# On-chip tensors begun at multiples of 512 bytes by fill words, in a fused two-block transformer kernel

## What is computed

```python
def swiglu(x, w1, w3, w2):
    return (jax.nn.silu(x @ w1) * (x @ w3)) @ w2

def moe_swiglu(x, router_w, w1, w3, w2):
    ...
    logits = (xt @ router_w).astype(jnp.float32)
    top_vals, top_idx = lax.top_k(logits, TOP_K)
    ...
    for e in range(N_EXPERTS):
        out = out + combine[:, e:e + 1] * swiglu(xt, w1[e], w3[e], w2[e])
```

## The kernel before

| tile | before | after |
|---|---|---|
| `raw`, `whi`, `wlo`, `h`, `tok`, `xh`, `xl`, `con` | 128 | 0 |
| `kc2`, `xw`, `bias` | 416 | 0 |
| `qT`, `kT`, `vs`, `ob`, `sg`, `pT`, `zt`, `postg` | 288 | 0 |
| `qk`, `sq` | 416 | 0 |
| `v2`, `qkT`, `uT` | 32 | 0 |
| `cv`, `mixT`, `mixs`, `spa`, `spb`, `wT` | 64 | 0 |
| `gt`, `ht`, `pt_in`, `hTh`, `hTl`, `ptTh`, `ptTl`, `pg`, `pm` | 416 | 0 |
| `mTh`, `mTl`, `xnh`, `xnl`, `xgh`, `xgl`, `yh`, `yl`, `pick`, `pickT` | 416 | 0 |
| `kd`, `xwh` | 352 | 64 |
| `xwl` | 128 | 352 |
| `cmpa`, `cmpb` | 480 | 64 |

## Time and profile before

### The profile page before, as it was taken

One profiled execution on the slowest core, in us unless ns is written; L12 is line 12 of the kernel. 1 busy time (PEld: TensorE's weight loads), 2 busy tenths in 40 slices (PEclk: granted clock), 3 DMA queues, 4 the chain that ended last, 5 costly groups with the idle time before them and its releaser, 6 DMA issues.

```text
span 1925.3 us, 26803 instructions
## 1 busy us (share of the span) xinstructions
PE 1838.6 (95%) x9562; PEld 1546.2 (80%) x9562; DVE 1395.7 (72%) x1653; ACT 1220.0 (63%) x1536; POOL 5.9 (0%) x13
## 2 busy tenths in 40 slices
PE   8999979989999989879999999999999999999997
PEld 7877758979998779768878878788788787887885
DVE  4456755746664466458899898898998898989884
ACT  5545544644444455548687777786877777768773
POOL 0000000000000000000000000000000000000000
PEclk9889989999999999879999999999999999999999
DMA  9743223425445344219989899899898998998980
GB/s 321 248 165 109 74 102 131 154 100 190 177 190 202 111 175 176 93 67 339 369 319 362 317 364 364 310 367 355 325 361 319 352 360 325 358 345 343 357 323 23
DMA packets 68336, 483.32 MB, mean 251 GB/s; under 512 B 7610, under 2 KB 7738, under 8 KB 10928
## 3 DMA queue, kind: packets, MB, share of 16 engines
q1 hardware_dynamic: 66480, 475.26, 64.9%
q0 software_dynamic: 1792, 7.18, 1.8%
HBM read 478.22 MB, written 4.19 MB: 251 GB/s over the span
## 4 chain that ended last, share of the span: by engine, by line
PE 80%; DVE 8%; ACT 6%; issue 5%; DMA 0%; ACTq 0%; DVEq 0%; POOLq 0%
PE ps L1471 20%; PE ps L1472 19%; PE ps L1476 19%; DVE wlo L892 4%; PE ps L1716 4%; PE ps L1723 4%; PE ps L1717 4%; PE ps L1454 3%; ACT whi L549 2%; PE ps L1928 1%; PE ps L1929 1%; ACT xgh L846 1%; DVE sg L1015 1%; ACT sg L672 1%; PE ps L1819 1%
## 5 line engine op out<-in xcount | busy, mean ns | idle before, releaser
L892 DVE TENSOR_TENSOR wlo<-raw,whi 128x1024 fp32r<-128x1024 f32 x906 | 1044.1, 1212 | 171.8 <-ACT whi L549 171.3
L549 ACT ACTIVATE whi<-raw 128x1024 fp32r<-128x1024 f32 x906 | 904.2, 1055 | 154.6 <-PE ps L1476 127.4
L1471 PE MATMUL ps<-whi,xgh 128*128 128x512 f32 x896 | 360.2, 402 | 4.6 <-ACT whi L549 4.6
L1472 PE MATMUL ps<-whi,xgl 128*128 128x512 f32 x896 | 355.0, 396 | 0.0
L1476 PE MATMUL ps<-wlo,xgh 128*128 128x512 f32 x896 | 282.2, 396 | 0.0
L1471 PE MATMUL ps<-whi,xh 128*128 128x512 f32 (+1 forms) x448 | 186.9, 418 | 21.9 <-issue 9.9
L1471 PEld LDWEIGHTS ps<-whi,xgh 128*128 128x128 f32 x896 | 168.9, 188 | 43.1 <-ACT whi L549 4.8
L1476 PEld LDWEIGHTS ps<-wlo,xgh 128*128 128x128 f32 x896 | 168.9, 188 | 40.8
L1472 PEld LDWEIGHTS ps<-whi,xgl 128*128 128x128 f32 x896 | 169.2, 189 | 37.8
L1472 PE MATMUL ps<-whi,xl 128*128 128x512 f32 (+1 forms) x448 | 181.3, 406 | 0.0
L1471 PE MATMUL ps<-whi,mTh 128*128 128x512 f32 x448 | 178.3, 398 | 0.0
(11 more groups left out here) (288 smaller groups left out, 1902.5 us busy)
## 6 DMA issues: line engine op xcount, KB each, us to landing
raw<-in_w_moe_dram SPq DMA_DIRECT2D x336, 1024.0 KB, 6.7
raw<-in_w_fixed_dram SPq DMA_DIRECT2D x112, 1024.0 KB, 4.9
bias_scratch<-revb POOLq DMA_DIRECT2D x1, 3072.0 KB, 39.2
bias<-bias_scratch POOLq DMA_DIRECT2D x1, 2048.0 KB, 18.2
raw<-in_w_fixed_dram SPq DMA_DIRECT2D x4, 512.0 KB, 4.2
tok<-in_xt_dram SPq DMA_DIRECT2D x2, 512.0 KB, 4.5
h<-in_x_dram SPq DMA_DIRECT2D x1, 1024.0 KB, 13.6
out_dram<-h SPq DMA_DIRECT2D x2, 512.0 KB, 2.8
```

The source lines that it names most:

```text
L549: AC(whi[:, v % SPL, c], raw[:, v % RAW, c], ACT.Copy).then_inc(high_done, 1)
L892: V.tensor_tensor(wlo[:, v % SPL, c], raw[:, v % RAW, c], whi[:, v % SPL, c].bitcast(F32), ALU.subtract).then_inc(low_done, 1)
L1471: mm(o, hi(k0 + k, T), wh[:, k, :], start=first and k == 0, stop=False)
L1472: mm(o, lo(k0 + k, T), wh[:, k, :], start=False, stop=False)
```

## The change

A helper `fill` allocates a tile that nothing uses, as long as is missing to the next multiple of 512 bytes. It is called at four places: ahead of `raw`, after `con`, after the small tiles common to all stages, and after the small tiles of the attention stage. `cbias`, `cu` and `qk_ss`, whose sizes are no multiples of 512, are allocated later than before, behind the large tiles of their scopes. All engines run the same instructions in the same order, on other addresses.

```diff
--- before.py
+++ after.py
@@ -47,6 +47,8 @@
 
 SMALL_PARTS = (("gains", 7 * KD), ("square", 7 * P), ("tril", 64), ("diag", 8), ("ogain", 2 * KD), ("qkg", 4),
                ("convw", 32), ("rw", KD * NE))
+LINE = 512
+FRONT = 16512
 SMALL = {}
 SMALL_WORDS = 0
 for _name, _n in SMALL_PARTS:
@@ -136,6 +138,12 @@
         def sb(name, shape, dt=F32, scope=ctx):
             return scope.enter_context(nc.sbuf_tensor(name, shape, dt))
 
+        def fill(name, used, scope=ctx):
+            used = -(-used // 32) * 32
+            if used % LINE:
+                sb(name, [P, (LINE - used % LINE) // 4], scope=scope)
+
+        fill("front", FRONT)
         raw = sb("raw", [P, RAW, KU * NB])
         whi = sb("whi", [P, SPL, KU * NB], F32R)
         wlo = sb("wlo", [P, SPL, KU * NB], F32R)
@@ -144,6 +152,7 @@
         xh = sb("xh", [P, KD, S], F32R)
         xl = sb("xl", [P, KD, S], F32R)
         con = sb("con", [P, SMALL_WORDS])
+        fill("con_end", 4 * SMALL_WORDS)
 
         def part(name):
             a, n = SMALL[name]
@@ -161,6 +170,7 @@
         st = sb("st", [P, 64])
         epst = sb("epst", [P, 1])
         nround = sb("nround", [1, 1], I32)
+        fill("common_end", 512 + 256 + 32 + 32)
 
 
         with ExitStack() as nsa:
@@ -172,10 +182,10 @@
                 xw = sb("xw", [P, XT], scope=a)
 
             bias = sb("bias", [P, NH, S], scope=nsa)
-            cbias = sb("cbias", [P, NT, NH, NC_], scope=nsa)
             qT = sb("qT", [P, NH // 2, S], scope=nsa)
             kT = sb("kT", [P, 2, NG, S], scope=nsa)
             vs = sb("vs", [P, 2, NT, NG * DH], scope=nsa)
+            cbias = sb("cbias", [P, NT, NH, NC_], scope=nsa)
             cmpw = sb("cmpw", [P, CB + 6 * DH], scope=nsa)
             pos2 = cmpw[:, 0:CB].rearrange("p (a m) -> p a m", a=2)
             w2k = cmpw[:, CB:CB + 4 * DH].rearrange("p (j s d) -> p j s d", j=2, s=2)
@@ -185,6 +195,8 @@
             cst = sb("cst", [P, 3, NT * NH], scope=nsa)
             grow = sb("grow", [P, NT, NH], scope=nsa)
             ast_ = sb("ast", [P, 16, 3, RG], scope=nsa)
+            fill("nsa_end", 4 * (NT * NH * NC_ + CB + 6 * DH + NG * NC_ + NT * 3 * NH + 3 * NT * NH + NT * NH
+                                 + 16 * 3 * RG) + 16, scope=nsa)
             with ExitStack() as early:
                 with ExitStack() as a:
                     oh = sb("oh", [NBUCK + 1, 512 + LREV + NH], scope=a)
@@ -215,11 +227,9 @@
         with ExitStack() as mx:
             qk = sb("qk", [P, 2, NT, NB], scope=mx)
             sq = sb("sq", [P, NT, NB], scope=mx)
-            qk_ss = sb("qk_ss", [P, 2, NT, SH], scope=mx)
             v2 = sb("v2", [P, NT, NB], scope=mx)
             qkT = sb("qkT", [P, 2, 4, S], scope=mx)
             uT = sb("uT", [P, 4, S], scope=mx)
-            cu = sb("cu", [P, 4, S + 2], scope=mx)
             cv = sb("cv", [P, 4, S], scope=mx)
             mixT = sb("mixT", [P, 8, S], scope=mx)
             mixs = sb("mixs", [P, 8, S], scope=mx)
@@ -228,6 +238,8 @@
             spa = sb("spa", [P, 4, 3 * P], scope=mx)
             spb = sb("spb", [P, 4, 3 * P], scope=mx)
             wT = sb("wT", [P, 4, 3 * P], scope=mx)
+            cu = sb("cu", [P, 4, S + 2], scope=mx)
+            qk_ss = sb("qk_ss", [P, 2, NT, SH], scope=mx)
 
 
         with ExitStack() as ff:
```

## The result

The changed kernel takes 1904.54 us (median of 4 runs, 1902.64 to 1906.22). The kernel before, run again beside it, takes 1923.38 (4 runs, 1921.16 to 1926.49). The ratio is 0.9898, with an interval of 0.9885 to 0.9911, so 18.8 us are gone, clear of the interval. The forecast was 1899.4 and a ratio of 0.989. Against the 1921.33 shown ahead of the prediction, which three runs gave, the 1904.54 lies 0.9% lower. The profiled executions differ by a little more: 1927.16 before, 1906.07 after (span 1904.3), 21.1 us.

The account below looks back on a forecast made before the run. The prediction took TensorE's stream as the bound (95% busy, 80% of the chain). Expert loop 19.4, dense w2 2.2 and `ple` 0.3 sum to 21.9 us, taking 1921.33 to 1899.4 us; range 1893 to 1923.

Parts of the forecast that it names:

- 1.36 and 2.72 between the groups: Sign: `wlo` matmul groups 1.36 us apart in the expert loop instead of 1.40, 2.72 in dense w2 instead of 2.80.
- 2.72 in the `xh` blocks still: Sign: 12 matmuls with stationary tile `xh`/`xl` keep taking 2.72 us, as before the change.
- 0.96 us for eight of `unit_T`: Sign: eight `unit_T` matmuls, with stationary tile `whi`/`wlo`, keep taking 0.96 us.
- the condition: In `products`: a stationary tile 32 bytes off a 64-byte multiple, the moving tile not, costs 6.67 ns per matmul.
- Rival 2: Address 0 is a bad start, so `xh`/`xl` and `unit_T` matmuls slow by 21.4 us, to 1942.7; chance 0.07.
- rival 3: Full multiple removes another 6.67 ns of the 13.3 above 213.3 everywhere, 45.8 us more, to 1853.6; chance 0.04.
- The expert loop: Eight rounds of 127.68 us, each 2.4 us shorter after the restart cost, 19.4 us in all.
- 96 matmuls after the gather: VectorE sets the end there, so 0.64 us won on PE returns as a longer wait for `yl`: nothing.
- The restarts: After transposes in the expert loop, nine a round, streams take time to settle: 0.3 us a round, between 0 and 1.0.
- From the scatter to the next gather's end, 408 matmuls, PE is held by no one: In each expert round, 408 matmuls at 6.67 ns gain 2.72 us, since VectorE still idles in each hidden block.
- Dense w2: 336 matmuls with `hTh`/`hTl`, PE busy 50.0 of 50 us, at 6.67 ns each: 2.2 us gained.
- `ple`: Two stages of 24 matmuls each with `ptTh`/`ptTl`, the last work on PE there: 0.3 us, nothing if hidden.

Follow-up runs that it names:

- E1: Changed kernel with the stationary tiles moved to 32 bytes past a multiple of 512, weight rings left at 0: 1923.69 us, ratio to before 0.9996.
- E2: Changed kernel with 32 bytes more fill ahead of all tiles, so stationary and moving tiles both begin at 32: 1904.96 us, ratio to before 0.9902.
- E4: Changed kernel with the weight rings, `xh` and `xl` moved to 32, stationary tiles of expert loop and dense w2 at 0: 1922.41 us.
- E3: Kernel before with 32 bytes of fill ahead of `gt`, stationary tiles at 448, rings at 128, distance 320: 1923.01 us, ratio to before 0.9996.
- E5: Changed kernel with `hTh` 256, `xgh` 128, `mTh` 64 and `ptTh` 16 bytes from the rings, which stay at 0: 1921.85 us, one run.
- E8: Changed kernel with VectorE's split of the round's last unit moved behind the two `yl` instructions: 1900.73 us, ratio to before 0.9877.
- E9: Changed kernel with VectorE's `pick` made earlier and its last split moved behind the two `yl`: 1893.94 us, ratio to before 0.9839.

## Why the prediction was right

**The mechanism.** The reading of the trace of before held: one form of matmul took 226.7 ns in one stage and 233.3 in another, and what sorted them was an address. All signs that the prediction named came: 1.36 and 2.72 between the groups, 2.72 in the `xh` blocks still, 0.96 us for eight of `unit_T`, 1219 and 1060 ns on VectorE and ScalarE, and the 16 transposes in 1.91 us. The round is 125.60 us, where about 125.3 was named. E1, E2 and E4 show the cause, which before was argued from three stages only. What the prediction had wrong is the condition. It blamed a stationary tile "32 bytes off a 64-byte multiple while the moving tile doesn't"; E3 and E5 show that distances of 64, 128 or 320, all multiples of 64, are as slow. Both conditions give the same answer for this change, since it puts everything at 0. That the number didn't suffer from the wrong condition is luck. For a change that had set the tiles at 64-byte multiples, the same reasoning would have missed by the whole gain, as E3 does.

**Rival 2 (0 is a bad start)** and **rival 3 (a full multiple gives still more)** have fallen with the same rows: the `xh` blocks go from 128, 128 to 0, 0 and stay at 2.72, `unit_T` stays at 0.96, and E2 reaches the time of after with everything at 32.

**The expert loop.** Forecast 2.4 us a round, measured 2.07 (seven rounds), 16.6 in eight where 19.4 was forecast. The terms, each by its own row:
- 96 matmuls after the gather gain nothing: right. VectorE's stretch kept its length, gather to scatter is 27.01 us as before, and the wait for `yl` went to 1.36 us, forecast 1.4. E8 confirms it from the other side: relieve VectorE there of one unit's split (2.27 us), and 0.91 us a round comes out.
- The restarts, taken as 0.3 us a round: right in size. In the chain before, from one group of transposes to the second `wlo` group behind it is 2.76 us; after, it is 2.76 too at one place. The matmuls right behind transposes gain little. Over a stretch of 120 matmuls with three such restarts the chain goes from 29.08 us (1115.89 to 1144.97) to 28.39 (1107.65 to 1136.04), 0.69 less where 120 x 6.67 ns is 0.80; the 0.11 lost is 0.04 each, and nine are 0.3.

The chain around one of these restarts, before, then after:

```profile
1131.98 0.44 PE ps L1454 x4
...
1134.74 0.47 PE ps L1476 x2
```

```profile
1123.31 0.44 PE ps L1466 x4
...
1126.07 0.45 PE ps L1488 x2
```

- "From the scatter to the next gather's end, 408 matmuls, PE is held by no one": this step failed, at one place. I had looked at VectorE's idle time inside the hidden blocks and not at the last thing that TensorE needs from it ahead of the gather, `pick`, which stands behind the splits in VectorE's queue. The trace of before had a sign of it: 0.75 us from the pair's start to the gather, where two matmuls of 0.23 take 0.46, and a gather that begins 0.13 us after `pick` ends. PE was held there already, and that place swallowed 0.26 us a round, 2.1 in eight. With 408 x 6.67 = 2.72, less 0.3 for restarts and 0.26 for `pick`, 2.16 are left. Measured are 2.07 by the `xgh` pieces, and 2.08 from the scatter's first matmul to the next gather's (100.67 to 98.59).

**Dense w2 and the rest.** Dense w2 went from 2.80 to 2.72 for 12. From its first matmul to its last group of four it was 78.33 us (579.93 to 658.26) and is 76.18 (576.09 to 652.27): 2.15 less, forecast 2.2. `ple` had 48 matmuls at the new price, 0.3 us; no comparison here resolves that. The sum of the parts is 16.6 + 2.2 + 0.3 = 19.1 us, and the medians differ by 18.8.

The spans of the two profiled executions differ by 21.0 us, in four parts: 3.8 ahead of dense w2, 2.15 in it, 1.5 lost again between it and the first matmul with `xgh`, and 16.5 from there to the end (857.28 to 1925.3 before, 852.77 to 1904.3 after). The 3.8 is no gain of the change: dense w2 begins anywhere between 574.01 us (E2) and 579.93 (before), and in E9, with matmuls as quick as after, it begins at 579.67.

So the forecast's 21.9 us was 3 us too much, nearly all in the term of the expert loop, and the median that it was taken from was 2 us lower than what more runs of the kernel before give. In the time both go the same way, 1904.54 against 1899.4; the ratio, 0.9898 against 0.989, is free of the second.

## What to carry to other kernels

If one form of matmul has two prices in two stages, sort the stages by what differs, start addresses included. For fp32r with 512 columns, let the moving and the stationary tile begin at the same place modulo 256 bytes, and watch odd-sized small tiles ahead of large ones, since any of them shifts all that follow. When the engine that bounds gets faster, look for every point in its loop where it needs something from an engine with a full queue. A listed wait isn't the only sign: see also what ends just ahead of each change of work. A small result queued behind bulk work (`pick`, `yl`) can be moved forward without touching the bulk; here that brought 0.69 and 0.91 us a round.

## What the runs showed of the hardware that was not expected

In unbroken streams a matmul of 512 columns in fp32r took 233.3 ns instead of 226.7 when the stationary tile's start differed from the moving tile's by 32, 64, 128, 288 or 320 bytes, and 226.7 when by 0 or 256 (all modulo 512). Equal starts of 0, 32 and 128 were alike. The weight load's own mean was 188 ns at either price. `unit_T`, with 256 columns, took 120 ns each throughout, but in all these kernels both tiles of `unit_T` begin at the same place modulo 512, so what it would pay at another distance isn't shown. For transposes one case is: the stationary tiles `kc2` and `tok`, at 416 and at 128 with the moving tile at 128, both took 1.91 us for 16. On VectorE and ScalarE no start tried changed the large operations by more than 3 ns (128x1024: 1219 to 1221 and 1060 to 1063). Why it is 6.67 ns, which is 16 cycles of 2.4 GHz, and what makes up the 13.3 ns that rival 3 asked about, no run here tells.
